# Expert-coefficient placing: one compare for both one-hot tiles of four tokens, the softmax weights multiplied in by ScalarE

## The reference, cut to what matters

```
top_s, top_i = lax.top_k(sc, PEER_TOPK)            # per head and half: 16 of 128 keys
cand_s = top_s[..., 0, :, None] + top_s[..., 1, None, :]
best_s, best_pos = lax.top_k(cand_s, PEER_TOPK)    # 16 of 256 pairs
idx = take_along_axis(cand_i, best_pos)            # i0 * 128 + i1
g = softmax(best_s)
act = gelu(einsum('phkd,pd->phk', expert_u[idx], xb))
coef = g * act
out = einsum('phk,phkd->pd', coef, expert_v[idx])
```

## Time and profile before

| | us |
|---|---|
| median of three runs | 2875.2 (2871.78 to 2875.94) |
| profiled execution, its own time | 2875.23 |
| its span, first to last instruction | 2873.9 |
| TensorE busy | 2716.1 (95%) |
| weight loads of TensorE busy | 2160.4 (75%) |
| VectorE busy | 1593.6 (55%) |
| ScalarE busy | 903.3 (31%) |
| GpSimd busy | 443.3 (15%) |
| mean granted TensorE clock | 0.964 of 2.4 GHz |

### The profile page before, as it was taken

One profiled execution on the slowest core, in us unless ns is written; L12 is line 12 of the kernel. 1 busy time (PEld: TensorE's weight loads), 2 busy tenths in 40 slices (PEclk: granted clock), 3 DMA queues, 4 the chain that ended last, 5 costly groups with the idle time before them and its releaser, 6 DMA issues.

```text
span 2873.9 us, 30823 instructions
## 1 busy us (share of the span) xinstructions
PE 2716.1 (95%) x11980; PEld 2160.4 (75%) x11980; DVE 1593.6 (55%) x3009; ACT 903.3 (31%) x1297; POOL 443.3 (15%) x228
## 2 busy tenths in 40 slices
PE   3989987979899999999999999999999999999998
PEld 2776876868688888888888888887876557788887
DVE  7864698888985334443344566554643454533332
ACT  4433332323243223322233333333232232322221
POOL 5334322323221000000000000004300002111100
PEclk9989998989999999999999999999998899999999
DMA  6533243444356333333333454522221001222232
GB/s 240 198 117 115 91 137 120 156 138 147 120 162 207 126 123 125 116 106 126 122 125 143 165 212 175 191 88 88 81 75 65 1 1 52 79 98 96 95 94 83
DMA packets 140720, 344.53 MB, mean 120 GB/s; under 512 B 8800, under 2 KB 74464, under 8 KB 135840
## 3 DMA queue, kind: packets, MB, share of 16 engines
q1 hardware_dynamic: 137184, 294.06, 29.7%
q0 software_dynamic: 3392, 48.50, 4.4%
HBM read 292.19 MB, written 50.33 MB: 119 GB/s over the span
## 4 chain that ended last, share of the span: by engine, by line
PE 69%; DVE 3%; DMA 1%; ACT 0%; issue 0%; DVEq 0%; POOLq 0%; ACTq 0%
PE bank L396 20%; PE bank L392 20%; PE bank L393 20%; PE bank L665 2%; PE bank L520 1%; PE bank L645 1%; PE bank L636 1%; PE bank L634 1%; PE bank L641 1%; PE bank L643 1%; PE bank L652 1%; DVE one_hot L1451 1%; PE bank_stat L418 0%; PE bank L409 0%; DMA weight<-expert_coefs 0%; DVE one_hot L1446 0%
## 5 line engine op out<-in xcount | busy, mean ns | idle before, releaser
L392 PE MATMUL bank<-h_lo,weights_hi 128*128 128x512 f32 x2176 | 882.4, 406 | 34.8 <-ACT weights_hi L732 31.4
L393 PE MATMUL bank<-h_hi,weights_hi 128*128 128x512 f32 x2176 | 871.4, 400 | 0.0
L732 ACT ACTIVATE weights_hi<-weights_raw 128x1024 fp32r<-128x1024 f32 (+1 forms) x411 | 431.1, 1049 | 508.7 <-PE bank L396 415.5
L396 PE MATMUL bank<-h_hi,weights_lo 128*128 128x512 f32 x2176 | 555.7, 396 | 3.1 <-DVE weights_lo L1145 3.1
L392 PEld LDWEIGHTS bank<-h_lo,weights_hi 128*128 128x128 f32 x2176 | 418.2, 192 | 139.1 <-ACT weights_hi L732 31.7
L393 PEld LDWEIGHTS bank<-h_hi,weights_hi 128*128 128x128 f32 x2176 | 417.7, 192 | 98.1 <-issue 0.2
L396 PEld LDWEIGHTS bank<-h_hi,weights_lo 128*128 128x128 f32 x2176 | 409.9, 188 | 103.3 <-DVE weights_lo L1145 3.6
L1748 POOL TENSOR_TENSOR weights_lo<-weights_raw,weights_hi 128x1024 fp32r<-128x1024 f32 x128 | 317.0, 2480 | 928.3 <-ACT weights_hi L732 928.3
L1145 DVE TENSOR_TENSOR weights_lo<-weights_raw,weights_hi 128x1024 fp32r<-128x1024 f32 (+1 forms) x283 | 359.0, 1271 | 35.3 <-ACT weights_hi L732 34.6
L1339 DVE SCALAR_TENSOR_TENSOR residual<-bank,ada,residual 128x512 f32<-128x512 f32 x136 | 102.2, 752 | 408.0 <-PE bank L396 407.9
L392 PE MATMUL bank<-mixed_lo,weights_hi 128*128 128x512 f32 x768 | 299.0, 389 | 0.0
(11 more groups left out here) (304 smaller groups left out, 2547.5 us busy)
## 6 DMA issues: line engine op xcount, KB each, us to landing
weights_raw<-in_expert_u SPq DMA_DIRECT2D x128, 512.0 KB, 3.4
weights_raw<-in_expert_v SPq DMA_DIRECT2D x128, 512.0 KB, 3.2
expert_coefs<-stage SPq DMA_DIRECT2D x32, 1024.0 KB, 6.3
weight<-expert_coefs POOLq DMA_DIRECT2D x16, 2048.0 KB, 8.8
ada_raw<-in_w_ada SPq DMA_DIRECT2D x40, 512.0 KB, 4.5
hidden_store<-hidden SPq DMA_DIRECT2D x14, 1024.0 KB, 5.9
hidden<-hidden_store POOLq DMA_DIRECT2D x7, 2048.0 KB, 14.2
weights_raw<-in_w_ffn_gate SPq DMA_DIRECT2D x22, 512.0 KB, 3.2
```

Of the source, the lines that this page charges most:

```text
L392: M.matmul(bank[:], hi[:, c:c + P], m_lo[k], start=start and i == 0, stop=False)
L393: M.matmul(bank[:], hi[:, c:c + P], m_hi[k], start=False, stop=False)
L396: ins = M.matmul(bank[:], lo[:, c:c + P], m_hi[k], start=False, stop=stop and i == len(tiles) - 1)
L732: S.activation(w_hi[n % SPLIT][:, 0:w], w_raw[n % RAW][:, 0:w], ACT.Copy).then_inc(*hi_done.inc(n))
```

## The change

make_hot becomes one compare of 128 x 1024 elements, which makes both one-hot tiles of four tokens, without weights. A new ScalarE function, weigh, multiplies the weights in, in place: four activations (Copy with a scale operand from chosen_t), one per token. Placing waits for the fourth of them instead of for VectorE. In ScalarE's program each quad's weigh takes the place of its copy from the bank, and that copy (placed) comes one quad later, after the next weigh; the last one of the stage follows ahead of the last block's Gelu.

```diff
@@ -514,7 +514,7 @@
 
             def place(tb, quad):
                 bank = take(("place", tb, quad))
-                M.wait_ge(*dve["hot", tb, quad])
+                M.wait_ge(*act["weighted", tb, quad])
                 hot = one_hot[quad % N_HOT]
                 for t in range(4):
                     ins = M.matmul(bank[:, t * P:(t + 1) * P], hot[:, 0, t, :], hot[:, 1, t, :], start=True, stop=True)
@@ -942,6 +942,15 @@
                              banks["place", tb, quad][:].rearrange("p (t n) -> p n t", t=4), ACT.Copy) \
                     .then_inc(*act.inc(("place", tb, quad)))
 
+            def weigh(tb, quad):
+
+                S.wait_ge(*dve["hot", tb, quad])
+                for t in range(4):
+                    at = 4 * quad + t
+                    hot = one_hot[quad % N_HOT][:, 1, t, :]
+                    S.activation(hot, hot, ACT.Copy, scale=chosen_t[tb % 2][:, 2, at:at + 1]) \
+                        .then_inc(*act.inc(("weighted", tb, quad) if t == 3 else ("weighted", tb, quad, t)))
+
             for j in range(FIRST_U):
                 hidden_gelu(j)
             soften(0)
@@ -950,7 +959,11 @@
                 if n == SOFTEN_AT and tb + 1 < TB:
                     soften(tb + 1)
                 for quad in range(first, end):
-                    placed(tb, quad)
+                    weigh(tb, quad)
+                    if (tb, quad) > (0, 0):
+                        placed(*((tb, quad - 1) if quad else (tb - 1, QUADS - 1)))
+                if (tb, n) == (TB - 1, PLACE_U[TB - 1] - 1):
+                    placed(tb, QUADS - 1)
                 if n == PLACE_U[tb] - 1 and tb + 1 < TB:
                     turned(tb + 1)
                 hidden_gelu(placed_block(tb, n))
@@ -1442,15 +1455,9 @@
                     V.wait_ge(*pe["place", tb, quad - N_HOT])
                 elif tb:
                     V.wait_ge(*pe["place", tb - 1, QUADS - N_HOT + quad])
-                steps[0] += 1
-                V.tensor_tensor(hot[:, 0], placed[:, 0, t0:t0 + 4].unsqueeze(2).broadcast_to([P, 4, P]),
-                                const("iota").unsqueeze(1).broadcast_to([P, 4, P]), ALU.is_equal) \
-                    .then_inc(*dve.inc(("step", steps[0])))
-                for t in range(4):
-                    steps[0] += 1
-                    V.tensor_scalar(hot[:, 1, t, :], const("iota"), placed[:, 1, t0 + t:t0 + t + 1],
-                                    placed[:, 2, t0 + t:t0 + t + 1], ALU.is_equal, ALU.mult) \
-                        .then_inc(*dve.inc(("hot", tb, quad) if t == 3 else ("step", steps[0])))
+                V.tensor_tensor(hot[:], placed[:, 0:2, t0:t0 + 4].unsqueeze(3).broadcast_to([P, 2, 4, P]),
+                                const("iota").unsqueeze(1).unsqueeze(1).broadcast_to([P, 2, 4, P]), ALU.is_equal) \
+                    .then_inc(*dve.inc(("hot", tb, quad)))
 
             router = route_tokens(0)
             for h in range(HEADS):
```

## The result

The changed kernel takes 2993.9 us (median of four runs, 2990.8 to 2995.6) where the kernel before takes 2874.6: ratio 1.0415 with a 95% interval of [1.0397, 1.0433], 119 us slower. The forecast was 3028 us, in a range of 2970 to 3090. The whole difference arises in the placing stage.

The account below looks back on a forecast made before the run. TensorE, busy 95%, was taken as the bound, with placing waiting 60.3 us for VectorE. ScalarE's chain and softmaxes gave 620 us, lost clock 50 and 5: stage 675 against 521.8, +153, so 3028 us, range 2970 to 3090.

Parts of the forecast that it names:

- The term that decides: Placing stage: Gelu, four multiplies and handoff delay each block's first quad 2.14 us; further quads come every 1.70 us.
- The softmax term: After three softmaxes in the placing stage, the first quad waits 6.13 us instead of 2.14, 12 us in all.
- The clock term: TensorE falls to half speed after new gaps in two thirds of 53 blocks, 1.42 us each: 50 us, plus 5 after softmaxes.
- rival 1: No loss of TensorE clock in the placing stage: +98 us, 2973 us; chance 0.13 down to no drop.
- The other signs: Profile after: placing waits 165 us for multiplies in nearly all 128 quads; VectorE busy about 300 us, waiting for placing.
- What costs nothing: Later coefficient stores and weight loads, PSUM's seven banks, GpSimd's low-half subtraction and the stage's last copies add no wait.
- Rival 2: ScalarE's in-place instructions don't overlap: 2.20 us per further quad, 2.54 for the first; +237 us, 3112 us; chance 0.08.
- rival 4: Weighing is off placing's path, tiles reused or weighed earlier: 2796 us; chance 0.02, shared with Rival 3.
- Rival 3: ScalarE's multiplies run beside the products, stage 443 us: -79 us, 2796 us; chance 0.02, shared with rival 4.

Follow-up runs that it names:

- the first experiment: Changed kernel with ScalarE's multiplies for block j+1 issued before the Gelu of block j, copies with their own quad, exponential earlier: 2811.1 us, 0.978 of the kernel before.

## Why the prediction was right, and where its size was off

**The term that decides.** The first quad's wait was put at 2.14 us, the distance of further quads at 1.70, a block of two quads at 10.37; measured were 2.12 (10.31 less 1.64, 0.88 and 5.67), 1.64 to 1.65, and 10.31. The multiplies take 391 ns and 0.29 us between starts instead of 0.40 and 0.30. The estimate from the page ScalarE: Activation LUTs of the Trainium skill (section What ACT_TABLE_LOAD costs), 386 ns and 293 between starts, is closer to this trace than my sum from an exponential. All blocks at full clock make 45 x 10.32 + 6 x 11.97 + 5 x 13.63 - 2.1 (the last block has no successor) = 602 us; forecast 608. By experiment it is the order that costs, not the work.

**The softmax term** (3 x 4.0) was right. After product 11 of the first group:

```profile
505.70 0.60 ACT L918 ACTIVATE hidden<-bank 128x512 f32<-128x512 f32 x1 [5.49 <-PE bank L396]
...
507.61 0.31 ACT L924 ACTIVATE chosen<-chosen 128x128 f32<-128x128 f32 x1
...
508.83 3.50 DVE L1458 TENSOR_TENSOR one_hot<-chosen_t,consts 128x1024 f32<-128x1024 f32 x3
510.09 1.28 ACT L951 ACTIVATE one_hot<-one_hot,chosen_t 128x128 f32<-128x128 f32 x4 [2.17 <-DVE one_hot L1458]
...
511.51 0.77 PE L520 MATMUL bank<-one_hot 128*128 128x128 f32 x2 [5.85 <-ACT one_hot L951]
```

6.0 us from the product's end (505.50) to placing, forecast 6.13. Between Gelu and the exponential lies a table load of ScalarE of 1.28 us (ACT_TABLE_LOAD at 506.31), as it did before. A block that takes 10.32 takes 14.23 here.

**The clock term was mis-sized.** I took two of three places of before as the share of the 53 blocks that fall to half speed: 50 us, and 5 for the three blocks after a softmax. Measured against blocks at full clock it is 25 us in all. The three blocks after a softmax (12, 28 and 44) lose 5.5, as forecast. Of the 53 others 19 lose the clock, and 19.5 us by it: ten in the first three groups 12.9 us (1.1 to 1.6 each), the three that come second after a softmax (13, 29 and 45) 2.8 us, and six of the last group 3.8 us (0.4 to 0.7 each). So the share was 19 of 53 and not 35, and a loss was 1.0 us on average and not 1.42. That is 30 of the 35 us by which the stage was forecast too long (675 against 640). One such block, with the clock of a later stretch of one us:

```profile
463.64 1.13 PE L520 MATMUL bank<-one_hot 128*128 128x128 f32 x8 [1.94 <-ACT one_hot L951]
465.29 1.54 PE L520 MATMUL bank<-one_hot 128*128 128x128 f32 x8 [0.52 <-ACT one_hot L951]
466.49 0.77 PE L392 MATMUL bank<-h_lo,weights_hi 128*128 128x512 f32 x1
...
469.46 0.40 PE L393 MATMUL bank<-h_hi,weights_hi 128*128 128x512 f32 x1
```
```profile
467.00:468.00 1.00, 1.00 (x4) 0.75 (x3) 0.97 (x2) 0.00 (x0) 1.00 (x1) 0.50 0.97 272
```

The gaps before its quads are the same 1.94 and 0.52 us as in the block at 534, where nothing fell. Three places were too few for a share of fifty. My argument against rival 1, that the new gaps are longer (2.98 against 2.48 us), set two measures side by side: 2.98 counts from when TensorE could have gone on, 2.48 is idle time of the profile. In idle time of the profile the new gaps are 1.94 + 0.52 = 2.46 us, no longer than at the three places. Rival 1, no loss at all, gave 2973 and was nearer than my 3028; the measured 2994 lies between the two.

**The other signs.** The waits were 149.4 us in 108 pieces where 165 in nearly all 128 were forecast. VectorE was busy for 356 us in the stage and not for about 300; the wide compare is 31 of that (188 instead of 157, held up by GpSimd, see the last section), the rest was not taken apart. ScalarE waited for a compare only at the stage's start and after the softmaxes, four times and 8.8 us in all.

**What costs nothing** did: no wait of TensorE in the stage names the weights or one of the seven PSUM banks that the kernel hands out, and after the stage the wait for L1158's low halves is 3.5 us instead of 3.1, so stores and loads one quad later cost nothing that can be told from none. **Rival 2** (no overlap on ScalarE) is out by 0.29 us between starts, **rival 4** (weighing off the path) by the 149.4 us of waits that name it. **Rival 3** described the kernel that the first experiment made: 2796 was its price, 2811 was measured and 2800 with the routing spread. The rule of the Trainium skill (Perfetto Trace Analysis, section Optimizing Scalar/DVE Operations) that a saturated VectorE may hand work to ScalarE holds here once the work stands before the wait, and the changed kernel shows what it costs when it doesn't. What stays open is why some blocks lose the clock and others with the same gaps keep it.

## What to carry to other kernels

Before work is moved to an idle engine, read that engine's program order: what the work stands behind in its queue comes on the consumer's path, however idle the engine is. Here Gelu waits for product j, so all that stands behind it waits too; the same instructions made the kernel 119 us slower there and 63 us faster one block earlier. A chain of few terms, each from a timeline of before, gave the block to 0.1 us; a term built on the share of three events was off by two and a half times (50 us against 19.5), and belongs in the range, not in the middle value.

## What was not expected of the hardware

The wide compare, a TENSOR_TENSOR with two broadcast operands, was held up by GpSimd: 1226 ns at the median, 1490 on average, 3430 at the longest. Of the 128 compares 21 took over 1350 ns, each of them while a subtraction of GpSimd ran; the 80 beside no subtraction took 1228 at most. One case, VectorE and GpSimd:

```profile
527.17 2.40 POOL L1755 TENSOR_TENSOR weights_lo<-weights_raw,weights_hi 128x1024 fp32r<-128x1024 f32 x1 [9.58 <-ACT weights_hi L732]
527.40 3.25 DVE L1458 TENSOR_TENSOR one_hot<-chosen_t,consts 128x1024 f32<-128x1024 f32 x1 [0.62 <-PE bank L520]
```

The compare is issued while GpSimd's subtraction (527.17 to 529.57) runs, and ends 1.08 us after it, at 530.65, not far from the 1.21 us that it takes at the least: its own work was done after the subtraction. The Trainium skill (SBUF — State Buffer, section Who interferes with whom) says that a VectorE instruction with two SBUF inputs contends with a GpSimd instruction that reads SBUF, and that contention on the ports they share is an exclusive lock. This trace agrees: 3.25 us instead of 1.23, done 1.08 us after the subtraction. Before, the one-hots of 128 elements with scalars from a column showed most of these hold-ups (465 ns on average for a median of 339; those beside no subtraction took 346 at most). In the changed kernel they are hidden behind ScalarE; with the exponential moved they are what is left of a wait (1.50 us above).

Half speed during a placing is hidden in the changed kernel, since 1.65 us per quad is about what a slow placing needs (two in 3.35 us in the block at 475.54), and is fully paid where ScalarE waits for the placing (3.94 instead of 3.06 us).
